# First MLP layer of a decoder trunk with the weights as stationary operand: more and narrower matmuls, no transposes, the row factor squared behind the second layer

## The reference, cut to what matters

```python
def rms_norm(x, gain):
    xf = x.astype(jnp.float32)
    y = xf * lax.rsqrt(jnp.mean(xf * xf, axis=-1, keepdims=True) + NORM_EPS)
    return (y * gain.astype(jnp.float32)).astype(x.dtype)
...
        h = rms_norm(x, norm2_g[l])
        x = x + jnp.square(jax.nn.relu(h @ w_ff_up[l])) @ w_ff_down[l]
    return rms_norm(x, final_norm_g)
```

## Time and profile before

| what | value |
|---|---|
| median of 3 runs | 1839.65 us |
| profiled execution, its own time | 1839.5 us |
| profiled execution, span of the core | 1837.7 us |
| granted TensorE clock over the span | 0.999 |
| TensorE busy | 1818.1 us (99%) |
| VectorE busy | 1086.0 us (59%) |
| ScalarE busy | 883.4 us (48%) |
| first MLP layer, first half, from its first transposes to the last | 1144.66 to 1303.24 us |

### The profile page before, as it was taken

The page is one execution under the profiler, slowest core; times in us unless marked ns, Lnnn a source line. Parts: engine busy times, 40 slices in busy tenths (PEclk is TensorE's granted clock), DMA queues, the critical chain, the costliest instruction groups (busy, mean ns, idle before and its releaser), DMA issues.

```text
span 1837.7 us, 29585 instructions
## 1 busy us (share of the span) xinstructions
PE 1818.1 (99%) x10928; PEld 1479.4 (81%) x10928; DVE 1086.0 (59%) x1531; ACT 883.4 (48%) x1388; POOL 115.4 (6%) x82
## 2 busy tenths in 40 slices
PE   7999999999999999999999999999999999999998
PEld 6888787787787877778888888888888888888886
DVE  5567686777766576665555555555544455555454
ACT  6464454554644555555444455444433344444443
POOL 0022031040220000000000000000000000000110
PEclk9999999999999999999999999999999999999999
DMA  6543443434434544445656655555555555555554
GB/s 252 173 160 124 142 145 120 150 127 139 149 127 139 182 152 152 151 158 161 205 194 200 206 199 189 188 185 183 193 192 193 192 192 184 185 187 187 194 195 138
DMA packets 88020, 316.33 MB, mean 172 GB/s; under 512 B 9712, under 2 KB 10224, under 8 KB 87792
## 3 DMA queue, kind: packets, MB, share of 16 engines
q1 hardware_dynamic: 87056, 312.58, 50.9%
q0 software_dynamic: 576, 2.10, 0.3%
q10 hardware_dynamic: 288, 0.18, 0.1%
HBM read 312.72 MB, written 2.10 MB: 171 GB/s over the span
## 4 chain that ended last, share of the span: by engine, by line
PE 98%; DVE 0%; issue 0%; DMA 0%; ACT 0%; DVEq 0%; POOLq 0%; POOL 0%; SPq 0%; ACTq 0%
PE acc L325 30%; PE acc L326 29%; PE acc L327 29%; PE J L382 2%; PE J L421 1%; PE J L531 1%; PE J L413 1%; PE J L580 1%; PE J L591 1%; PE J L425 1%; PE J L389 1%; PE J L370 1%; PE J L544 1%; PE J L451 0%; PE J L554 0%
## 5 line engine op out<-in xcount | busy, mean ns | idle before, releaser
L1159 DVE TENSOR_TENSOR w_lo<-raw,w_hi 128x1024 fp32r<-128x1024 f32 x584 | 715.7, 1231 | 506.8 <-ACT w_hi L780 506.1
L780 ACT ACTIVATE w_hi<-raw 128x1024 fp32r<-128x1024 f32 x584 | 617.0, 1060 | 605.4 <-PE acc L327 602.7
L325 PE MATMUL acc<-w_hi,hT_hi 128*128 128x512 f32 x1440 | 579.8, 403 | 5.8 <-DVE hT_lo L1177 4.2
L326 PE MATMUL acc<-w_lo,hT_hi 128*128 128x512 f32 x1440 | 562.8, 391 | 0.0
L327 PE MATMUL acc<-w_hi,hT_lo 128*128 128x512 f32 x1440 | 562.3, 391 | 0.0
L325 PEld LDWEIGHTS acc<-w_hi,hT_hi 128*128 128x128 f32 x1440 | 270.8, 188 | 72.7 <-issue 11.2
L327 PEld LDWEIGHTS acc<-w_hi,hT_lo 128*128 128x128 f32 x1440 | 270.9, 188 | 58.1
L326 PEld LDWEIGHTS acc<-w_lo,hT_hi 128*128 128x128 f32 x1440 | 271.3, 188 | 52.1 <-issue 1.0
L325 PE MATMUL acc<-w_hi,act_hi 128*128 128x512 f32 x512 | 199.3, 389 | 0.0
L327 PE MATMUL acc<-w_hi,act_lo 128*128 128x512 f32 x512 | 199.2, 389 | 0.0
L326 PE MATMUL acc<-w_lo,act_hi 128*128 128x512 f32 x512 | 199.2, 389 | 0.0
(11 more groups left out here) (231 smaller groups left out, 1446.0 us busy)
## 6 DMA issues: line engine op xcount, KB each, us to landing
raw<-weights SPq DMA_DIRECT2D x584, 512.0 KB, 3.3
xres<-x SPq DMA_DIRECT2D x4, 512.0 KB, 7.3
xres<-x POOLq DMA_DIRECT2D x4, 512.0 KB, 5.8
y<-nat SPq DMA_DIRECT2D x8, 256.0 KB, 3.1
fgain_sb<-fgain SPq DMA_DIRECT2D x1, 1024.0 KB, 5.6
masks_sb<-masks SPq DMA_DIRECT2D x1, 576.0 KB, 10.7
zs<-w_ba SPq DMA_DIRECT2D x1, 256.0 KB, 9.2
dist_sb<-dist SPq DMA_DIRECT2D x1, 192.0 KB, 3.3
```

The source lines that it names most:

```text
L325: mm(o, aT_hi[:, kt, tok], w_hi[:, c % RING, w], start=first, stop=False)
L326: mm(o, aT_hi[:, kt, tok], w_lo[:, c % RING, w], start=False, stop=False)
L780: A(w_hi[:, slot], raw[:, slot], ACT.Copy).then_inc(hi_ready, 1)
L1159: tt(w_lo[:, slot], raw[:, slot], w_hi[:, slot].bitcast(F32), ALU.subtract).then_inc(lo_ready, 1)
```

## The change

The first layer's product has its operands exchanged. The weights are now stationary (128 input channels x 128 output channels, four column groups m of a chunk's block) and all 256 tokens move, so an output comes out channel-major, four 128 x 256 tiles in the same two PSUM banks, in the layout in which the second layer wants it. The transposes into `J` and their waits go; ScalarE and VectorE split the squares straight from `rbuf` in SBUF. With channels on partitions the row factor can't be a scale per partition any more: it is left out of the ReLU and the square, GpSimd squares it once (`SQUARED`, counts `r_sq`), and VectorE multiplies each second-layer output by it as it adds it to `xres`.

```diff
-            def up_out(p, c0, prev, free, before=None, first=None):
-                def job(h):
-                    if first is not None:
-                        first(h)
-                    if prev is not None and h == 2:
-                        pe.wait_ge(relu_sq, prev)
-                        if not isinstance(prev, int) or prev > 1:
-                            pe.wait_ge(act_lo_done, prev - 1)
-                        turn_group(rbuf[:, 1 - p], 2 * (1 - p), up_T)
-                output(c0, 1 - p, hT_hi, hT_lo, free, job, before=before)
+            def up_out(p, c0, free, before=None, jobs=None):
+                for c in range(CPO):
+                    if before:
+                        before(c)
+                    pe.wait_ge(lo_ready, c0 + (c + 1))
+                    if c == 0:
+                        for s_free, v in free:
+                            pe.wait_ge(s_free, v)
+                    for k in range(CK):
+                        kt = c * CK + k
+                        for m in range(4):
+                            w = slice(k * NB + m * P, k * NB + (m + 1) * P)
+                            o = acc[:, 1 - p, m // 2, (m % 2) * T:(m % 2 + 1) * T]
+                            mm(o, w_hi[:, c % RING, w], hT_hi[:, kt], start=(kt == 0 and m % 2 == 0), stop=False)
+                            mm(o, w_lo[:, c % RING, w], hT_hi[:, kt], start=False, stop=False)
+                            last = mm(o, w_hi[:, c % RING, w], hT_lo[:, kt], start=False, stop=(kt == KT - 1 and m % 2 == 1))
+                        if k == CK - 1:
+                            last.then_inc(chunk_used, 1)
+                        if jobs:
+                            jobs(kt)
...
                 def last_T(h):
-                    if h == 2:
-                        pe.wait_ge(relu_sq, r0 + FF_UP)
-                        pe.wait_ge(act_lo_done, r0 + FF_UP - 1)
-                        turn_group(rbuf[:, 1], 2, up_T)
...
@@ ScalarE: relu, up_job
                     if not skip:
-                        act.wait_ge(up_T, k)
-                    if skip and k < 0:
-                        act.wait_ge(r_x, 4)
-                    for t in range(NT):
-                        ins = A(rbuf[:, p, t], acc[:, par, t], ACT.Relu, scale=row_scale(1, t))
+                        act.wait_ge(act_lo_done, k)
+                    for b in range(2):
+                        ins = A(rbuf[:, p, b], acc[:, par, b], ACT.Relu)
...
                     if h == 2:
-                        act.wait_ge(up_T, cnt)
-                        for b in range(2):
-                            ins = A(act_hi[:, bass.ds(kt + 2 * b, 2), :], J[:, b0 + b].rearrange("p (a t) -> p a t", a=2), ACT.Copy)
-                        ins.then_inc(act_hi_done, 1)
+                        act.wait_ge(relu_sq, cnt)
+                        A(act_hi[:, bass.ds(kt, 4), :].rearrange("p a t -> p (a t)"), rbuf[:, p].rearrange("p b n -> p (b n)"),
+                          ACT.Copy).then_inc(act_hi_done, 1)
...
@@ VectorE: add_x, square, up_job, last output
+                        if row is not None:
+                            dve.wait_ge(r_sq, 1)
                         for t in range(NT):
                             dst = xres[:, t, col]
-                            ins = tt(dst, dst, acc[:, par, t], ALU.add)
+                            if row is None:
+                                ins = tt(dst, dst, acc[:, par, t], ALU.add)
+                            else:
+                                ins = stt(out=dst, in0=acc[:, par, t], scalar=row_scale(row, t), in1=dst,
+                                          op0=ALU.mult, op1=ALU.add)
...
-                    for t in range(NT):
-                        ins = stt(out=rbuf[:, p, t], in0=acc[:, 1 - p, t], scalar=row_scale(1, t), in1=rbuf[:, p, t],
-                                  op0=ALU.mult, op1=ALU.mult)
+                    for b in range(2):
+                        ins = tt(rbuf[:, p, b], acc[:, 1 - p, b], rbuf[:, p, b], ALU.mult)
...
                         dve.wait_ge(act_hi_done, cnt)
-                        for b in range(2):
-                            ins = tt(act_lo[:, bass.ds(kt + 2 * b, 2), :], J[:, b0 + b].rearrange("p (a t) -> p a t", a=2),
-                                     act_hi[:, bass.ds(kt + 2 * b, 2), :].bitcast(F32), ALU.subtract)
-                        ins.then_inc(act_lo_done, 1)
+                        hi, lo = (o[:, bass.ds(kt, 4), :].rearrange("p a t -> p (a t)") for o in (act_hi, act_lo))
+                        tt(lo, rbuf[:, p].rearrange("p b n -> p (b n)"), hi.bitcast(F32), ALU.subtract).then_inc(act_lo_done, 1)
...
-                tt(xres[:, t, w3], xres[:, t, w3], acc[:, 1 - (FF_DOWN - 1) % 2, t], ALU.add).then_inc(half_added, 1)
+                stt(out=xres[:, t, w3], in0=acc[:, 1 - (FF_DOWN - 1) % 2, t], scalar=row_scale(SQUARED, t),
+                    in1=xres[:, t, w3], op0=ALU.mult, op1=ALU.add).then_inc(half_added, 1)
...
@@ GpSimd
             row_factor(1)
+            pool.wait_ge(r_x, 4)
+            tt(stat[:, 16 + 2 * SQUARED:18 + 2 * SQUARED], stat[:, 18:20], stat[:, 18:20], ALU.mult).then_inc(r_sq, 1)
```

More of the change, by code:

```diff
@@ L183, in row_scale @@
             return stat[:, 16 + 2 * k + t:17 + 2 * k + t]
-        Q_SCALE, GATE_SCALE = 3, 4
+        Q_SCALE, GATE_SCALE, SQUARED = 3, 4, 5
         RH = mats[:, M_B0].rearrange("p u c -> p (u c)")
@@ L276, in hybrid_trunk @@
         gate_done, merged, merge_link = sem("gate_done"), sem("merged"), sem("merge_link")
-        relu_done, relu_sq, up_T, act_hi_done, act_lo_done = (
-            sem(n) for n in ("relu_done", "relu_sq", "up_T", "act_hi_done", "act_lo_done"))
+        relu_done, relu_sq, r_sq, act_hi_done, act_lo_done = (
+            sem(n) for n in ("relu_done", "relu_sq", "r_sq", "act_hi_done", "act_lo_done"))
         x_added, y_dve, y_act, y_out = sem("x_added"), sem("y_dve"), sem("y_act"), sem("y_out")
@@ L739, in _ @@
                 for p in range(2):
-                    up_out(p, c0 + p * CPO, (r0 + p) if p else None, [(x_added, x0 - 1 + p)],
+                    up_out(p, c0 + p * CPO, [(x_added, x0 - 1 + p)],
                            *((turned_by(2), turn_last(2, x_added, 4)) if hf == 0 and p == 0 else ()))
@@ L744, in _ @@
                     for p in range(2):
-                        up_out(p, i * (2 * CPO) + (c0 + p * CPO), i * 2 + (r0 + p), [(relu_sq, i * 2 + (r0 + p - 1))])
+                        up_out(p, i * (2 * CPO) + (c0 + p * CPO), [(relu_sq, i * 2 + (r0 + p - 1))])
                 cd = c0 + FF_UP * CPO
                 def last_T(h):
-                    if h == 2:
-                        pe.wait_ge(relu_sq, r0 + FF_UP)
-                        pe.wait_ge(act_lo_done, r0 + FF_UP - 1)
-                        turn_group(rbuf[:, 1], 2, up_T)
                     if h == 27:
@@ L1104, in ops, with up_job @@
                     if not skip:
-                        act.wait_ge(up_T, k)
-                    if skip and k < 0:
-                        act.wait_ge(r_x, 4)
-                    for t in range(NT):
-                        ins = A(rbuf[:, p, t], acc[:, par, t], ACT.Relu, scale=row_scale(1, t))
+                        act.wait_ge(act_lo_done, k)
+                    for b in range(2):
+                        ins = A(rbuf[:, p, b], acc[:, par, b], ACT.Relu)
                     ins.then_inc(relu_done, 1)
                 return ops
-            def up_job(b0, kt, cnt):
+            def up_job(p, kt, cnt):
                 def job(h):
                     if h == 2:
-                        act.wait_ge(up_T, cnt)
-                        for b in range(2):
-                            ins = A(act_hi[:, bass.ds(kt + 2 * b, 2), :], J[:, b0 + b].rearrange("p (a t) -> p a t", a=2), ACT.Copy)
-                        ins.then_inc(act_hi_done, 1)
+                        act.wait_ge(relu_sq, cnt)
+                        A(act_hi[:, bass.ds(kt, 4), :].rearrange("p a t -> p (a t)"), rbuf[:, p].rearrange("p b n -> p (b n)"),
+                          ACT.Copy).then_inc(act_hi_done, 1)
                 return job
@@ L1133, in _ @@
                         q = i * 4 + (q0 + 2 * p)
-                        output(q, up_job(2 * (1 - p), i * 8 + 4 * (p - 1), i * 2 + (r0 + p)),
+                        output(q, up_job(1 - p, i * 8 + 4 * (p - 1), i * 2 + (r0 + p)),
                                read(q + 2, relu(p, 1 - p, i * 2 + (r0 + p - 1), False)))
@@ L1137, in _ @@
                 for n in range(FF_DOWN):
-                    job = up_job(2, 28, r0 + FF_UP) if n == 0 else add_squares(n, 8, rbuf[:, 0]) if hf == 1 else None
+                    job = up_job(1, 28, r0 + FF_UP) if n == 0 else add_squares(n, 8, rbuf[:, 0]) if hf == 1 else None
                     output(qd + 4 * n, job, lambda: None, nch=2 * CPO)
@@ L1562, in _, with add_x @@
                 output(q + 2, None, read(q + 4, merge))
-            def add_x(col, back=None):
+            def add_x(col, back=None, row=None):
```

(4 more changed lines are left out.)

## The result

The changed kernel takes 1846.03 us (median of 6 runs, 1844.76 to 1846.72) against 1839.65 us: 0.32% slower, ratio 1.0032 with a 95% interval of 1.0021 to 1.0044. The forecast was 1825.4 us, its range 1824 to 1846 us. The profiled execution took 1846.05 us, its span is 1844.2 us.

A forecast was written before the change was run, and what follows sets the result against it. The prediction took TensorE's own instruction stream as the bound; -13.9 (transposes), -0.4 (matmuls behind them) and +0.06 us (last addition) gave -14.2 us, from 1839.5 to 1825.3, with the median's 0.15 1825.4 us; range 1824 to 1846 us.

The forecast's parts named there:

- The pace of a matmul: First layer on TensorE: a 256-column matmul with a fresh 128-column load takes 113.3 ns, half of 226.6.
- 1536 matmuls of 226.6 against 3072 of 113.3: 0: Term for the first layer's product: twice as many matmuls at half the time each, no change.
- The load is hidden: First-layer weight loads, recorded with 188 ns, overlap the matmul ahead and fit in 113.3 ns by some 3 ns.
- three readings: Trace rows on transposes, first loads behind them and one 256-column matmul: a load needs 0.11 us ahead of its matmul.
- third reading: A 256-column matmul at 49.57 us, followed by a full 128-column load, whose matmul starts at 49.69: a 0.12 us step.
- The rest of the sum: All terms except the product's pace: transposes, matmuls behind them, last addition, waits, splits, row factor and ring; -14.2 us.
- Rival 1: First-layer matmuls: the hand-over to a wide load costs more than 113.3 ns, up to 120 ns, 1846 us; chance 0.14.
- Rival 2: First-layer loads become the bound: 188 ns a step, 2055 us, or one after the other, 2163 us; chance 0.09.
- sentence on row groups: Skill page's rule that a weight load overlaps matmuls in flight only when their row groups differ; it spoke against the forecast.
- Rival 3: TensorE's instruction supply can't keep one instruction every 57 ns in the first layer; likely some tens of us; chance 0.04.
- estimate of 124 ns a pair: The skill page's 62 ns for issuing a matmul, counted for its load too: +33 us, 1858 us.
- Rival 4: The weight ring can't deliver the 4% faster first layer, so PE waits for what it saved: 1839.6 us; chance 0.03.

The follow-up runs named there:

- e3: The kernel before with only the operands of the first layer's product exchanged, transposes kept: 1859.78 us, ratio 1.0112.
- e2: The changed kernel with the first layer's product put back to stationary activations and 512 moving weight columns: 1825.37 us, ratio 0.9923.
- m1_grid: Separate kernel of only fp32r streams of 60 matmuls, by moving columns N and stationary columns W: 119.8 ns a step at N=256, W=128.
- e6: The changed kernel with first-layer stationary tiles of 64 instead of 128 columns, half the hidden channels left out: 1825.35 us, ratio 0.9924.

## Why the prediction was wrong

**The step that failed** is the one under "The pace of a matmul": 113.25 ns "is half of 226.6 within the resolution, so the two show no fixed part: time goes with the moving columns". The term "1536 matmuls of 226.6 against 3072 of 113.3: 0" measured +20.1 us alone (e3) and +20.7 us beside the rest (the changed kernel against e2). The equality was a coincidence of two shapes that differ in two ways. The 512-column stream takes about 13.3 ns beyond its columns behind a 128-column load, the 256-column stream of L616 takes 6.7 ns behind a 32-column one (m1_grid: 6.7 above N/2.4 for W=32, 13.2 for W=128 at the same N=256). Half the columns and half the extra look like a rate.

**The load is hidden: right.** The three readings said that a load needs 0.11 us ahead of its matmul; the streams with 192 and 128 moving columns put it at 111 ns. But that only rules the load out as the longer of two; it doesn't show that a matmul behind a wide load takes no longer. The third reading had the answer in it and was read too far: from 49.57 to 49.69 us are 0.12 us, and at a resolution of 0.01 us neither 113 nor 120 ns is excluded. With 3.1 us for each nanosecond the rows had to tell 3 ns apart and could not.

**The rest of the sum** (-13.9 for the transposes, -0.4 behind them, +0.06 at the end, nothing for waits, splits, row factor and ring): right as a sum, -14.3 us measured by e2; apart from the last addition no run measured its terms one by one. At the end of the changed kernel the last addition takes 0.75 us where it took 0.69:

```profile
1835.93 0.75 DVE L1627 SCALAR_TENSOR_TENSOR xres<-acc,stat,xres 128x512 f32<-128x512 f32 x1 [1.54 <-PE acc L327]
```

**The rivals.** Rival 1 is what happened, and at its upper end: a part of the step that comes with the wide load, 120.0 ns a step, 1846 us. Its chance of 0.14 was too low. The one difference between the two streams that no row had measured at N=256, the width of the load, was named as "where the whole forecast is decided"; and the equality of 2 x 113.25 and 226.6, set down against this rival, came from streams of different W and so said nothing of W=128 at N=256. Rival 2 (188 ns, or load and matmul in turn, 0.22 us) is excluded by the steps of 120.0 ns in the kernel and of 111 ns in m1_grid. The sentence on row groups that the prediction takes from the Trainium skill, page TensorE: Matmul & The Clock Gate, section Part 3 (The mechanism), goes with it for this kernel: loads over all 128 rows overlap the matmuls here. The same section also has loads pulled ahead when they target the array's background weight buffer, and that is what this trace agrees with. Rival 3 (instruction supply) is excluded by e6, which runs one instruction every 57 ns through whole outputs and loses nothing. The Trainium skill, same page, section Part 2, Decode and dispatch, gives its 62 ns for a matmul and not for a load, and steps of 113 to 120 ns can't test that; the prediction's estimate of 124 ns a pair, which counted the load too, is excluded by e6's 113.3 ns and by the 60.0 ns of the stream with N=128 and W=32. Rival 4 (the ring) didn't occur: PE waits for `w_lo` as little as before, 1.8 us in all against 1.5, and in e6, which has the forecast's pace, the stage draws 195 GB/s with PE busy throughout.

**What stays open** is the mechanism. The step at N=256 grows with W, the width of the stationary tile. W sets the width of the load and also the number of PSUM partitions that the matmul writes, and every matmul in every run has a load of its own (12336 and 12336 in the changed kernel), so no run shows which of the two costs the time; "the part that goes with the load" is a name for it, not a shown cause. A fixed part of some 13 ns fits N=256 to 416 behind wide loads within 1.6 ns; it doesn't explain 202.7 ns at N=448, 216.9 at N=480, the 229.8 and 231.7 ns of narrow loads at N=512, or the pairs of 347.9 to 353.3 ns. No experiment here looked below the level of steps.

## What to carry to other kernels

Exchanging the operands of a product keeps the columns and changes the number of loads: with N of 256 in place of 512 each matmul with its 128-column load brings its extra part for half the work, here 13 ns of every 120, and 3072 such steps ate 14 us of removed transposes and 6 us more. That a load is hidden behind a matmul doesn't yet say that the step costs nothing beyond its moving columns. Before a forecast that multiplies a step by thousands, ask in which operand shapes the two reference streams differ and how many nanoseconds they can resolve; if the answer is more than the break-even, the rivals deserve nearly equal chances.

## What the runs showed of the hardware that had not been expected

- In fp32r, behind 128-column loads, steps of 227.0 (512), 173.7 (384), 146.5 (320) and 119.8 ns (256), then no less than 111 ns for 192 and for 128 moving columns.
- At N=512 narrow loads make a stream slower, not faster: 229.8 ns with W=64 and 231.7 with W=32 against 227.0 and 227.3 with W=128 (one execution each).
- The order of mixed lengths matters: 353.3 ns for a pair of 512 and 256 in turn, 348.3 in groups of two, 350.8 in groups of four. In the kernel the same reordering was worth 4.3 us (1839.7 to 1835.43).
- The recorded busy time of weight loads reaches 100% at a step of 120.0 ns, 99% at 113.3 with the narrow tile, and 100% even at 173.7 (m1_grid with N=384, 10.30 of 10.30 us), and a stream with 192-ns load records still steps every 111 ns; it doesn't tell how near the loads are to being the bound.
